# First phase's cached scores behind the decay sums, a third buffer for value pages, and a reordered last norm

## The reference

```
layer 0:  p = h @ w_in + b_in;  y = (gelu(u) * spatial_gate(layer_norm(gelu(v))) * silu(z)) @ w_out + b_out
          x = layer_norm(alpha*x + (1+gate)*y)
shared:   k, v, f = x @ kv_w + kv_b;  logf = log_sigmoid(f);  c = cumsum(logf)
layer 1:  q, z = h @ fa_w_in + b
          logits = q k / 8 + c_q - c_k, causal;  o = softmax(logits) v       (samples: cached k, v, logf by page_table)
          x = layer_norm(alpha*x + (1+gate)*((o * silu(z)) @ fa_w_out + b))
```

## Time and profile before

| | us |
|---|---|
| median of 3 runs | 1756.75 (1756.01 to 1758.0) |
| profiled execution | 1756.58 |
| its span (first to last instruction) | 1755.1 |
| PE busy | 1644.6 (94%) |
| DVE, ACT, POOL busy | 1011.6, 624.5, 418.1 |
| granted clock of PE, mean | 0.976 |

### The profile page before, as it was taken

The page is one execution under the profiler, slowest core; times in us unless marked ns, Lnnn a source line. Parts: engine busy times, 40 slices in busy tenths (PEclk is TensorE's granted clock), DMA queues, the critical chain, the costliest instruction groups (busy, mean ns, idle before and its releaser), DMA issues.

```text
span 1755.1 us, 27850 instructions
## 1 busy us (share of the span) xinstructions
PE 1644.6 (94%) x10080; PEld 1427.2 (81%) x10080; DVE 1011.6 (58%) x1572; ACT 624.5 (36%) x980; POOL 418.1 (24%) x413
## 2 busy tenths in 40 slices
PE   6999999999999997999897999999999999979965
PEld 4899999999999997999875778787777777757742
DVE  3433353433433437225576888879797977679436
ACT  2222122112112116225452646363645545462221
POOL 0240010110110100001221626252534435250020
PEclk9999999999999999999998999999999999999987
DMA  8491112222222221324424241433323231243474
GB/s 363 158 315 36 48 61 88 81 72 89 78 72 93 74 73 56 106 96 132 140 76 134 83 121 61 120 89 107 105 84 97 84 91 65 61 133 132 158 287 191
DMA packets 85778, 197.90 MB, mean 113 GB/s; under 512 B 16899, under 2 KB 47235, under 8 KB 83923
## 3 DMA queue, kind: packets, MB, share of 16 engines
q1 hardware_dynamic: 73154, 141.97, 24.9%
q0 software_dynamic: 12560, 55.10, 9.0%
HBM read 171.31 MB, written 34.39 MB: 117 GB/s over the span
## 4 chain that ended last, share of the span: by engine, by line
PE 76%; DVE 9%; issue 5%; DMA 3%; ACT 3%; POOL 2%; POOLq 0%; SPq 0%; DVEq 0%; ACTq 0%
PE bank L1846 20%; PE bank L1847 19%; PE bank L1848 19%; PE bank L2213 2%; PE bank L1981 2%; PE bank L2167 2%; PE bank L2215 2%; PE bank L2214 2%; PE bank L2195 2%; PE bank L2194 1%; POOL p_lo L656 1%; DVE bank L1497 1%; DMA pages<-cache_v 1%; PE bank L1961 1%; PE bank L2070 1%
## 5 line engine op out<-in xcount | busy, mean ns | idle before, releaser
L1846 PE MATMUL bank<-h_hi,w_lo 128*128 128x344 f32 x1152 | 373.8, 324 | 8.1 <-DVE h_lo L1142 8.1
L1847 PE MATMUL bank<-h_lo,w_hi 128*128 128x344 f32 x1152 | 367.9, 319 | 0.0
L1848 PE MATMUL bank<-h_hi,w_hi 128*128 128x344 f32 x1152 | 367.7, 319 | 0.0
L656 POOL TENSOR_TENSOR p_lo<-parg,p_hi 128x512 fp32r<-128x512 f32 (+1 forms) x192 | 227.3, 1201 | 161.4 <-ACT p_hi L983 161.1
L1846 PEld LDWEIGHTS bank<-h_hi,w_lo 128*128 128x128 f32 x1152 | 217.0, 188 | 13.4 <-issue 9.1
L1846 PE MATMUL bank<-x_hi,w_lo 128*128 128x512 f32 x528 | 220.4, 417 | 1.0 <-DVE x_lo L1571 0.9
L1847 PEld LDWEIGHTS bank<-h_lo,w_hi 128*128 128x128 f32 x1152 | 217.0, 188 | 0.2 <-issue 0.2
L1848 PEld LDWEIGHTS bank<-h_hi,w_hi 128*128 128x128 f32 x1152 | 216.8, 188 | 0.0
L1848 PE MATMUL bank<-x_hi,w_hi 128*128 128x512 f32 x528 | 208.5, 395 | 0.0
L1847 PE MATMUL bank<-x_lo,w_hi 128*128 128x512 f32 x528 | 208.5, 395 | 0.0
L1846 PE MATMUL bank<-y_hi,w_lo 128*128 128x320 f32 (+2 forms) x512 | 177.5, 347 | 15.7 <-DVE w_lo L1100 8.6
(11 more groups left out here) (301 smaller groups left out, 2630.5 us busy)
## 6 DMA issues: line engine op xcount, KB each, us to landing
raw<-units SPq DMA_DIRECT2D x121, 512.0 KB, 3.6
scr_k<-cache_k POOLq DMA_DIRECT2D x32, 512.0 KB, 6.1
ada_ring<-w_ada SPq DMA_DIRECT2D x32, 512.0 KB, 3.3
pages<-cache_v POOLq DMA_DIRECT2D x32, 512.0 KB, 5.9
kpb<-scr_k SPq DMA_DIRECT2D x24, 512.0 KB, 4.1
ada_first<-w_ada SPq DMA_DIRECT2D x8, 1024.0 KB, 15.2
KX<-KA SPq DMA_DIRECT2D x32, 256.0 KB, 7.2
ckb<-scr_c POOLq DMA_DIRECT2D x16, 512.0 KB, 4.7
```

The costliest lines, as they stand in the source:

```text
L656: g.tensor_tensor(p_lo[:, r, off:HALF], parg[:, r, off:HALF], p_hi[:, r, off:HALF].bitcast(F32), ALU.subtract).then_inc(S("p_ready"), 1)
L1846: mm(out, lhs_lo, rhs_hi, start=first, stop=False)
L1847: mm(out, lhs_hi, rhs_lo, start=False, stop=False)
L1848: return mm(out, lhs_hi, rhs_hi, start=False, stop=last)
```

## The change

Three parts. (1) Phase 0: on SP the query's round trip and keys 0 come behind KX and weight block (1,0) and wait for both halves of `ckb`; on DVE the pairs of product and sum move one slot later, the fourth behind the last exponents. (2) Last phase: ACT takes the first half's sums before probabilities 4 and splits y2 0 and 1 after probabilities 5; DVE's y2_low 0 and 1 come after exponents 9 and 10. (3) A third free buffer for values (slot 4): sets 0, 1, 2 are used at n = 9, 10, 12; sets 3 to 5 are loaded during the projection, 6 and 7 behind it; POOL and no longer SP issues `fsw`, behind the pages; in the norm, PE has tiles 2, 3 and 4 behind sets 4, 5 and 7, the mask's matmuls before tile 5, the fsw matmuls before tile 6 and the fs_row matmuls before tile 7, and DVE's mask_o, gated_s, fs_row and the sums follow that order.

```diff
 pages = at("pages", [P, 4, NP, D], F32, R2)
+pages_r3 = at("pages_r3", [P, NP, D], F32, R3 + 20480)
 xb2 = at("xb2", [P, 2, T], F32, R3)
...
 MOVED = 16 * 2 * NS * NP
-VALUE_SLOT = (0, 1, 0, 1, 2, 3, 0, 1)
-VALUE_IN = {0: ("pages_in0", MOVED + 16 * NP), 1: ("pages_in1", 16 * NP), 2: ("pages_in0", MOVED + 32 * NP),
-            3: ("pages_in1", 32 * NP), 4: ("pages_in2", 32 * NP), 5: ("pages_in2", 32 * NP),
-            6: ("pages_in0", MOVED + 48 * NP), 7: ("pages_in1", 48 * NP)}
+VALUE_SLOT = (0, 1, 4, 0, 1, 4, 2, 3)
+VALUE_IN = {0: ("pages_in0", MOVED + 16 * NP), 1: ("pages_in1", 16 * NP), 2: ("pages_in4", 16 * NP),
+            3: ("pages_in0", MOVED + 32 * NP), 4: ("pages_in1", 32 * NP), 5: ("pages_in4", 32 * NP),
+            6: ("pages_in2", 32 * NP), 7: ("pages_in2", 32 * NP)}
+
+def value_page(n, g):
+
+    return pages_r3[:, g, :] if VALUE_SLOT[n] == 4 else pages[:, VALUE_SLOT[n], g, :]
 SCORED = 4 * KB
...
         load_b(j + 1, 0)
+        if isinstance(j, int) and j == 0:
+            for h in range(2):
+                sp.wait_ge(S(f"ckb_in{h}"), 16)
+            load_query(0)
+            sp.wait_ge(S("pages_in0"), MOVED)
+            load_keys(0, 0)
         load_b(j + 1, 1)
...
     sp.wait_ge(S("ln1_back"), TT)
-    load_query(0)
-    sp.wait_ge(S("pages_in0"), MOVED)
-    load_keys(0, 0)
     load_phase(0, True)
...
-    sp.wait_ge(S("r2_ready"), 2 * KB)
-    sp.wait_ge(S("lo_ready"), U_FS)
-    for b in range(KB):
-        sp.dma_start(fsw[:, b, :, :], units[U_FA - WB + b, :, :, :]).then_inc(S("fsw_in"), 16)
-
     for t in range(TT):
...
-        s, (odd, p) = VALUE_SLOT[n], divmod(n, NP)
+        odd, p = divmod(n, NP)
         for g in range(4):
             entry = (2 * g + odd) * NP + p
             page = pool.value_load(ptab[0:1, entry:entry + 1], min_val=0, max_val=cache_v.shape[0] - 1)
-            pool.dma_start(pages[:, s, g, :], cache_v[bass.ds(page, 1), :, :].rearrange("a p c -> p (a c)"))\
+            pool.dma_start(value_page(n, g), cache_v[bass.ds(page, 1), :, :].rearrange("a p c -> p (a c)"))\
                 .then_inc(S(VALUE_IN[n][0]), 16)
...
             pool.wait_ge(S("pages_used"), SCORED - 4 + 4 * n)
-        elif n < 4:
-            pool.wait_ge(S("pages_used"), SCORED + n - 1)
-        elif n == 4:
+        elif n == 2:
+            pool.wait_ge(S("pages_used"), SCORED + 1)
+        elif n < 6:
+            pool.wait_ge(S("pages_used"), SCORED + n - 2)
+        elif n == 6:
             pool.wait_ge(S("fa_mm"), 2 * KB)
-        elif n >= 6:
-            pool.wait_ge(S("pages_used"), SCORED + n - 3)
         load_values(n)
+    pool.wait_ge(S("r2_ready"), 2 * KB)
+    pool.wait_ge(S("lo_ready"), U_FS)
+    for b in range(KB):
+        pool.dma_start(fsw[:, b, :, :], units[U_FA - WB + b, :, :, :]).then_inc(S("fsw_in"), 16)
     for name, n in (("vn_out", 16), ("k_out", 16 * KB), ("v_out", 16 * KB), ("kqv_s_out", 16)):
...
         shift(j, 1)
+        if not more:
+            take_sums(j, 0)
         probs(j, 4)
         if more:
             evac(j + 1, 0, 0)
-        take_sums(j, 0)
-        if more:
+            take_sums(j, 0)
             split_hi(j + 1, 1)
         probs(j, 5)
+        if not more:
+            y2_high(0)
+            y2_high(1)
         probs(j, 6)
...
             kq_high(j + 1, 0)
-        else:
-            y2_high(0)
-            y2_high(1)
         probs(j, 11)
...
         later = not isinstance(j, int) or j > 0
+        late_keys = keys and not later
+        keys = keys and later
         take_samples(j, 2)
...
         z_evac(j, 1)
+        if late_keys:
+            score_mul(j, 0)
         if keys:
...
             invert(j - 1, 1, 1)
+        if late_keys:
+            score_sum(j, 0)
         if keys:
...
         invert(j, 0, 0)
+        if late_keys:
+            score_mul(j, 1)
         if keys:
...
         divide_o(j, 0)
+        if late_keys:
+            score_sum(j, 1)
         if keys:
...
         exponents(j, 9)
+        if not more:
+            y2_low(0)
+        if late_keys:
+            score_mul(j, 2)
         if keys:
             score_mul(j, 3)
         exponents(j, 10)
+        if late_keys:
+            score_sum(j, 2)
         if keys:
             score_sum(j, 3)
         if not more:
-            y2_low(0)
             y2_low(1)
...
             kq_low(j + 1, 0)
+            if late_keys:
+                score_mul(j, 3)
+                score_sum(j, 3)
         else:
...
     layer_norm_stats(1, TT)
-    for t in range(2, 5):
-        finish(t - 2)
-        layer_norm_stats(t, TT)
+    finish(0)
+    layer_norm_stats(2, TT)
+    finish(1)
+    layer_norm_stats(3, TT)
+    finish(2)
+    layer_norm_stats(4, TT)
+    mask_o()
     finish(3)
-    mask_o()
     layer_norm_stats(5, TT)
+    gated_s()
     finish(4)
-    gated_s()
     layer_norm_stats(6, TT)
-    finish(5)
     for h in range(2):
         dve.wait_ge(S("fs_used"), h + 1)
         v.tensor_copy(fs_row[:, h * 512:(h + 1) * 512], bank(6 + h)).then_inc(S("fs_row"), 1)
+    finish(5)
     layer_norm_stats(7, TT)
-    finish(6)
     dve.wait_ge(S("fs_used"), 3)
...
     norm_sum(rS[:, :, :], KB)
-    finish(7)
+    finish(6)
     norm_square(3, rS[:, :, :], KB, rS[:, :, :])
     norm_var(3)
+    finish(7)
     norm_out(3, KB, "ln_g", KB, "ln_b", rS[:, :, :]).then_inc(S("ys_ready"), 1)
...
                 mm(bank(6 + h), pd[:, :], vtok[:, h * 512:(h + 1) * 512], start=True, stop=False)
-        s, (odd, p) = VALUE_SLOT[n], divmod(n, NP)
+        odd, p = divmod(n, NP)
         pe.wait_ge(S(VALUE_IN[n][0]), VALUE_IN[n][1])
...
                 rows = slice(2 * H * g, 2 * H * (g + 1))
-                last = mm(bank(6 + h)[rows, :], PZ[:, p, 2 * g + odd, :], pages[:, s, g, h * 512:(h + 1) * 512],
+                last = mm(bank(6 + h)[rows, :], PZ[:, p, 2 * g + odd, :], value_page(n, g)[:, h * 512:(h + 1) * 512],
                           start=False, stop=n == NS - 1)
...
                 decode_weights()
-            if n == 11:
+            if n == 9:
                 decode_values(0)
+            if n == 10:
+                decode_values(1)
             if n == 12:
-                decode_values(1)
+                decode_values(2)
     pe.wait_ge(S("r2_ready"), 2 * KB)
     ln_forward(0, r2T, TT)
     ln_forward(1, r2T, TT)
-    for n in range(2, 6):
-        decode_values(n)
-        ln_forward(n, r2T, TT)
+    decode_values(3)
+    decode_values(4)
+    ln_forward(2, r2T, TT)
+    decode_values(5)
+    ln_forward(3, r2T, TT)
     decode_values(6)
     decode_values(7)
+    ln_forward(4, r2T, TT)
     pe.wait_ge(S("d_step"), 4)
...
     last.then_inc(S("d_o"), 1)
-    ln_forward(6, r2T, TT)
+    ln_forward(5, r2T, TT)
     pe.wait_ge(S("d_step"), 5)
...
         last.then_inc(S("fs_used"), 1)
-    ln_forward(7, r2T, TT)
+    ln_forward(6, r2T, TT)
     for h in range(2):
...
     last.then_inc(S("fs_used"), 1)
+    ln_forward(7, r2T, TT)
     sample_sum(3, 0)
```

## The result

The changed kernel takes 1742.37 us (median of 4 runs, 1739.4 to 1743.34), the kernel before in the same runs 1756.38 us (1755.21 to 1758.0): a ratio of 0.9916, 95% interval 0.9901 to 0.9932, so 14.0 us less. A second series gave 1743.37 us and 0.9931 (0.9914 to 0.9948). The profiled execution took 1739.4 us, its span 1737.9: 17.2 less than the span before; it was the fastest of the four.

A forecast was written before the change was run, and what follows sets the result against it. The prediction took the kernel to be bound mostly by TensorE's matmuls and its waits. Its terms, -9.1 + 0 - 1.5 + 1.9 - 9.3 = -18.0, took 1756.6 us to 1738.6 us, range 1731 to 1749.

The forecast's parts named there:

- the first phase: Phase 0, third peak: ckb lands earlier with query and keys behind it, so TensorE waits less; -9.1 us.
- the moved keys: Phase 0's later keys, products and sums: they fit in existing gaps; cost 0, at worst 3.7 us plus 2.8 of low clock.
- the tail: After the last product: fewer waits for pages, none of VectorE for y_out, earlier ys_out; -9.3 us, ends -6 and -12.
- the end at -13.1: Phase 0, third peak, best end of the term: no wait of TensorE left and the clock kept; -13.1 us.
- the wait at its first peak: Phase 1, first peak: a wait of TensorE there would show the forecast wrong; no size given.
- Last phase: Earlier sums and y2 splits remove TensorE's 2.5 us wait, 2.2 come back at y2_low 2; -1.5 us, ends 0 and -4.
- Output projection: Values 2 comes in front of the last r2T, 16 matmuls on a full TensorE, delaying the norm's start; +1.9 us.
- the waits for pages under 4 us: Tail: a sign of being right, TensorE's waits for value pages stay under 4 us in all.
- Only the tail pays: Rival: ckb's landing is set by KX, raw and k_out; first term -2, last phase 0, 1747 us; chance 0.20.
- fsw late on GpSimd's queue: Rival, tail: fsw issued by POOL lands late, in front of tiles 6 and 7; +6, 1744.6 us; chance 0.08.
- The key cycle: Rival: single buffer kpb makes VectorE, then TensorE, wait for key loads; 1764 us at 15 us landings; slower, chance 0.05.
- More: Rival: scr_c free and ckb in by 931.5, -13.1, last phase -4, rest as forecast; 1732 us; chance 0.13.

The follow-up runs named there:

- early_store: The changed kernel with only the 4 KB store scr_q back at its old place: 1748.97 us, ratio 0.9961 to the kernel before.
- last_only: The kernel before with only the last phase's part of the change: 1753.65 us, ratio 0.9998.
- tail_only: The kernel before with only part (3): third value buffer, fsw on POOL and the norm's order; 1753.73 us, ratio 0.9981.
- changed_again: The changed kernel run once more, unaltered, in a later series: 1743.37 us, ratio 0.9931 to the kernel before.
- tiles_ahead: The changed kernel with the norm's transposes, statistics and finishes further ahead of the samples' chain: 1727.81 us, ratio 0.9848 to the kernel before.
- fsw_on_sp: The changed kernel with fsw issued by SP ahead of the first y_out, not by GpSimd: 1749.9 us, ratio 0.9966 to the kernel before.

## Why the prediction came out as it did

The median is 3.8 us above the forecast and inside the range. Three terms were off, and not all the same way: the first phase gave 3.0 more than forecast, the moved keys cost 0.8 to 3.5 where I had 0, and the tail gave 5.5 less. That the total came so near is in part luck.

*First phase, forecast -9.1, measured -12.1.* The mechanism was right: scr_q held f_out and scr_c, and early_store shows it. The term was mis-sized in its last step. I let ckb share the DMA with KX, raw and k_out until 932.5; it was issued at 921.27, ahead of all four KX, and its halves landed 5.4 and 7.2 us after their issues, the first before VectorE came to the first minimum at 927.87, the second at 929.0 (930.6 by the clock of the profile before). VectorE waited 1.0 us ahead of the second minimum, which fits that landing:
```profile
929.22 0.30 DVE L1505 CUSTOM_DVE_ANT_0 bank<-bank,ckb 128x128 f32<-128x128 f32 x1 [1.00 <-issue]
```
TensorE did not stand for it and the clock stayed up, the case that I had as the end at -13.1.

*The moved keys, forecast 0, measured 0.8 to 3.5 us.* From `parg` to the last phase the three profiles with the keys at their old place (before, last_only, tail_only) take 573.3 to 573.5 us, the ten with the first phase's part 574.2 to 576.9. What I had checked held: VectorE never waits for kpb (landings below), and the fourth pair fits in the gap before the samples are taken, of which 1.75 us are left.
```profile
DMA to landing us min/median/max: 3.7/4.1/8.2
```
```profile
1006.38 0.29 DVE L1390 COPY samp<-bank 128x128 f32<-128x128 f32 x1 [1.75 <-PE bank L2099]
```
I had priced VectorE's work and the landings, and not GpSimd's. The samples are taken 1.0 us later after `parg` than before (53.5 us, 52.5 before). While VectorE multiplies the fourth pair, GpSimd's last two p_lo take 2.40 us (1.42 before), and TensorE waits 0.8 us for them, a wait that the kernel before does not have (timelines of VectorE and GpSimd, and waits of PE from 985 to 1008 us):
```profile
1001.89 1.37 DVE L1458 TENSOR_TENSOR kpb<-kpb,qb 128x1024 f32<-128x1024 f32 x1
1001.18 2.40 POOL L659 TENSOR_TENSOR p_lo<-parg,p_hi 128x128 fp32r<-128x128 f32 x2 [2.91 <-ACT p_hi L990]
PE bank L2242 <- POOL p_lo L659: 0.8, 1, 0.8
```
And raw block 3, now issued 0.6 us ahead of the next scr_q, lands after 10.6 us; I had 4.5, and before, issued 4.3 us ahead of it, it took 4.8. GpSimd waits for it although the DMA engines move nothing from 1004 on (DMA issues of 997.5 to 999.5 us, and GpSimd's timeline):
```profile
raw<-units SPq DMA_DIRECT2D x1, 512.0 KB, 10.6
1009.04 1.90 POOL L623 TENSOR_TENSOR w_sc<-raw,one_p 128x1024 f32<-128x1024 f32 x1 [5.46 <-DMA raw<-units]
```
In some profiles that is all; in changed_again TensorE also waits 1.4 us for the minimum at phase 1's peaks and the phase is 2.6 us longer than before, close to the wait at its first peak that I had named as a sign of being wrong. Which of the moved pieces makes that, and why it varies from run to run, stays open.

*Last phase, -1.5.* The 2.2 us behind y2_low 2 came, as forecast, with part of the low clock. The part by itself is within the noise of the runs.

*Output projection, +1.9.* Together with the last phase the stretch gave -0.4 against a forecast of +0.4; two profiles of the changed kernel differ there by 1.7 us (149.4 and 151.0). Apart, last_only takes 146.1 there and tail_only 151.7, against 149.8 and 147.6 in the two profiles with neither: the signs are as forecast, but with one profile of each the sizes are not shown.

*Tail, forecast -9.3, measured -3.8: the step that failed.* "The eighth goes at 1698.5 and lands at 1702.5" put the last page 10.8 us after the first statistics; TensorE could start only after 14.9. I had added 4.0 us to the last issue, as for a load by itself, when four of the seven before it were still under way: the first of the eight landed 3.8 us after its issue, the last 8.4. The 32 products behind took 6.4 us at the lower clock (5.5 in the forecast), so tile 4's statistics came at 22.4 in place of 16.8. All 5.6 us are there: from those statistics to ys_out I had forecast 37.3 us and 37.2 were measured. But those 37 us held waits of VectorE (7.6 us for transposes), which I took from the order as written without asking whether they had to be; tiles_ahead takes 12.8 us off the tail by order alone. Of the signs that I had named, the waits for pages under 4 us failed (6.7); scr_c's landing, y_lo's wait, y_out and kpb came as said, and ys_out was issued at 1736.05.

*Rivals.* Only the tail pays (0.20): the reverse is true. fsw late on GpSimd's queue (0.08): TensorE's wait there is 2.6 us and is for oS; GpSimd issued the eight in 4.24 us. The key cycle (0.05): no wait of VectorE for kpb; what the move of the keys did cost came another way. "More" (0.13) had the first phase right and the tail wrong.

## What to carry to other kernels

Where stores or loads land late although the DMA engines are idle, look for one scattered store issued around them, and put it behind whatever somebody waits for; 0.6 us behind may be too near, though that was seen in the profiles and not tried by itself. Of two bulk loads, put the one wanted later behind the other on the same queue: there it was free, issued among the others on another queue it cost 9.5 us. In a tail where two chains share TensorE and VectorE, let the independent work (here the next tiles' transposes) stand ahead of each product that waits for the other engine; that was worth 12.8 us of the tail here, more than any other edit of the tail.

## What was not expected of the hardware

One 4 KB store held the landing of 64 KB stores on another engine's queue from 2.2 us to 6.9 and 9.7 us, after their bytes had moved; issued 0.6 us behind a 512 KB load, a store like it goes with a landing of 10.6 us in place of 4.8. And the eight page loads moved slower than the fsw loads behind them: 287 to 375 GB/s from 1676 to 1684 with the DMA engines 0.93 to 1.05 busy, against 420 GB/s from 1688 on (above). Two windows of the changed kernel:
```profile
1676.00:1678.00 2.00, 2.00 (x20) 1.27 (x22) 1.50 (x3) 0.00 (x0) 1.07 (x2) 1.00 0.93 287
...
1682.00:1684.00 2.00, 2.00 (x20) 0.66 (x13) 1.97 (x4) 0.32 (x1) 1.38 (x4) 1.00 1.05 375
```
In fsw_on_sp, with fsw asked for beside them, the same stretch behind the first page (1680 to 1682 there) went at 416 GB/s, against 295 in the changed kernel (1678 to 1680). Why a busy engine moves less there was not tried and stays open.
